# Two-layer encoder trunk: the feed-forward output product with four pairs of k-tiles by seven block products instead of eight, and its weight splits moved to VectorE

## What is computed

```python
def swiglu(x, w1, w3, w2):
    return (jax.nn.silu(x @ w1) * (x @ w3)) @ w2      # w1, w3: 1024 x 2816; w2: 2816 x 1024

for layer in range(2):
    mix = ...                                         # layer 0: chunk attention + state space; layer 1: stick-breaking attention
    h = layer_norm(ALPHA * h + mix, ln_mix_g[layer], ln_mix_b[layer])
    ffn = swiglu(h, ffn_w1[layer], ffn_w3[layer], ffn_w2[layer])
    h = layer_norm(ALPHA * h + ffn, ln_ffn_g[layer], ln_ffn_b[layer])
```

## Time and profile before

| | us |
|---|---|
| runs of the kernel | 1172.32, 1173.63, 1175.81 |
| median | 1173.63 |
| profiled execution, first to last instruction (span) | 1170.8 |
| PE busy in it | 1151.3 |
| DVE busy in it | 801.2 |
| POOL busy in it | 614.9 |
| output stage of layer 0, from the first to the last of its matmuls | 449.8 to 561.5 |
| output stage of layer 1 | 1043.6 to 1163.5 |

### The profile page before, as it was taken

How to read it: one execution, slowest core, us unless ns; L and a number is a source line. 1 busy time by engine, 2 the same in 40 slices (tenths; PEclk the granted TensorE clock), 3 DMA queues, 4 the chain that set the end, 5 groups by cost and what they waited for, 6 DMA issues and landing times.

```text
span 1170.8 us, 19103 instructions
## 1 busy us (share of the span) xinstructions
PE 1151.3 (98%) x7533; PEld 1003.2 (86%) x7533; DVE 801.2 (68%) x1064; ACT 514.5 (44%) x813; POOL 614.9 (53%) x384
## 2 busy tenths in 40 slices
PE   7999999999999999999999999999999999999997
PEld 6877768999999998888887777777999999998886
DVE  8558652897888887442804787756978888874427
ACT  6335674354544444222335555523544445543220
POOL 5897614356676767444353222213566776674440
PEclk9999999999999999999999999999999999999999
DMA  7623415143333334232243121202533333343211
GB/s 209 184 78 98 119 59 188 60 118 106 91 109 109 109 109 144 90 105 93 79 137 90 55 64 45 72 1 72 145 96 104 91 114 103 109 140 111 92 54 72
DMA packets 154201, 117.84 MB, mean 101 GB/s; under 512 B 19280, under 2 KB 140152, under 8 KB 154112
## 3 DMA queue, kind: packets, MB, share of 16 engines
q1 hardware_dynamic: 154112, 116.62, 33.3%
HBM read 113.17 MB, written 3.43 MB: 100 GB/s over the span
## 4 chain that ended last, share of the span: by engine, by line
PE 93%; DVE 4%; ACT 1%; DMA 1%; issue 0%; SPq 0%; POOL 0%; DVEq 0%; ACTq 0%
PE ps L1840 18%; PE ps L1841 17%; PE ps L1842 17%; PE ps L1862 10%; PE ps L1864 10%; PE ps L1863 10%; PE ps L2321 2%; PE ps L2347 2%; PE ps L2332 2%; PE ps L1870 1%; PE ps L2095 1%; PE ps L2365 1%; PE ps L2106 1%; PE ps L2367 1%; PE ps L2366 1%; PE ps L2119 1%
## 5 line engine op out<-in xcount | busy, mean ns | idle before, releaser
L693 POOL TENSOR_TENSOR wlo<-raw,whi 128x1024 fp32r<-128x1024 f32 x113 | 275.7, 2448 | 387.5 <-ACT whi L811 386.8
L1840 PE MATMUL ps<-xhi,whi 128*128 128x256 f32 (+1 forms) x848 | 272.3, 321 | 0.0
L1842 PE MATMUL ps<-xhi,wlo 128*128 128x256 f32 (+1 forms) x848 | 267.2, 315 | 0.0
L1841 PE MATMUL ps<-xlo,whi 128*128 128x256 f32 (+1 forms) x848 | 267.1, 315 | 0.0
L811 ACT CAST whi<-raw 128x1024 fp32r<-128x1024 f32 x113 | 120.1, 1075 | 190.8 <-PE ps L1864 160.4
L1840 PEld LDWEIGHTS ps<-xhi,whi 128*128 128x128 f32 x848 | 161.9, 191 | 17.4 <-issue 6.4
L772 POOL TENSOR_TENSOR wlo<-raw,whi 128x512 fp32r<-128x512 f32 x114 | 173.3, 1546 | 0.6 <-ACT whi L1077 0.4
L1842 PE MATMUL ps<-thi,wlo 128*128 128x256 f32 x608 | 172.4, 284 | 0.0
L1841 PE MATMUL ps<-tlo,whi 128*128 128x256 f32 x608 | 172.4, 284 | 0.0
L1840 PE MATMUL ps<-thi,whi 128*128 128x256 f32 x608 | 172.4, 284 | 0.0
L1842 PEld LDWEIGHTS ps<-xhi,wlo 128*128 128x128 f32 x848 | 161.8, 191 | 10.3
(11 more groups left out here) (253 smaller groups left out, 2008.2 us busy)
## 6 DMA issues: line engine op xcount, KB each, us to landing
raw<-in_ffn_w SPq DMA_DIRECT2D x132, 512.0 KB, 3.8
raw<-in_odd_w_in SPq DMA_DIRECT2D x24, 512.0 KB, 3.8
raw<-in_even_w_in SPq DMA_DIRECT2D x16, 512.0 KB, 4.6
h<-in_x SPq DMA_DIRECT2D x8, 512.0 KB, 5.3
raw<-in_even_w_out SPq DMA_DIRECT2D x8, 512.0 KB, 4.0
raw<-in_odd_w_out SPq DMA_DIRECT2D x8, 512.0 KB, 3.5
bias<-rel_scratch SPq DMA_DIRECT2D x8, 256.0 KB, 3.8
out<-h SPq DMA_DIRECT2D x3, 512.0 KB, 2.6
```

Source lines behind the costliest of these rows:

```text
L693: eng.tensor_tensor(lo, raw_of(b), hi, ALU.subtract).then_inc(w_lo, 1)
L1840: eng.matmul(o_, w_hi_, x_hi_, start=start, stop=False)
L1841: eng.matmul(o_, w_hi_, x_lo_, start=False, stop=False)
L1842: return eng.matmul(o_, w_lo_, x_hi_, start=False, stop=stop)
```

## The change

Of the 22 k-tiles of an output product, eight (0 to 7) are taken together: tiles 0 to 3 as the left and 4 to 7 as the right part of G (each pair of a left and a right tile is one of the four pairs), the tokens in two halves of 256, w2's columns in two halves of 512. The 2 x 2 block product then has seven block products P1 to P7 in place of eight. It is worked in two batches b of two pairs (JOINED = 4, BATCHES = 2), so there are 14 joint units of twelve matmuls. The matmuls of a product differ from plain ones only in their operands: sums of G blocks (`1s`, `3s`, `N`, `L`, 128 x 2 x 256) and of w2 blocks (`3t`, `1t`, `2t`, `4t`, 128 x 1024), all made by DVE; the w2 sums lie where x was, in `t1`, `t2`, `t3`. Where a product belongs to several outputs it is not kept aside: it is left in the PSUM bank of one of them and read into h by DVE at the right moment (`read_part`, eight reads of 128 x 512 a layer, with ALPHA * h in the same operation), and the next product is added to it in the same bank. The norm then adds h with factor 1.

The other 14 k-tiles stay plain. Ten (eight in layer 1) are taken as half units: A, two k-tiles for the left columns, and B, the same two for the right ones, with 24 matmuls each; the others are full units F of 24 matmuls as before. A product called 5b1 is P5 of batch 1.

The weight splits of this stage, and of no other, go from POOL to DVE (`out_lower`); ACT's half is `out_upper`. There are two more loads a layer, since the lower right blocks of w2 are loaded twice. Orders, and which sums DVE makes behind which unit:

```diff
+FIRST_UNITS = 3
+JOINED = 4
+OUT_ORDER = (
+    "A0 1b0 1b1 5b0 A1 5b1 A2 6b0 6b1 4b0 A3 2b0 A4 7b0 7b1 4b1 2b1 B0 3b0 B1 3b1 B2 B3 B4",
+    "A0 1b0 1b1 5b0 A1 5b1 6b0 A2 6b1 4b0 2b0 A3 7b0 7b1 4b1 2b1 B0 3b0 B1 3b1 B2 B3 F8")
+SUMS_BEHIND = (
+    {1: "N0 1s1 3s1", 2: "N1 3t0 1t0 2t0", 3: "3t1 1t1 2t1", 7: "4t0 L0", 8: "L1", 12: "4t1"},
+    {1: "N0 1s1 3s1", 2: "N1 3t0 1t0 2t0", 3: "3t1 1t1 2t1", 6: "4t0 L0", 8: "L1", 11: "4t1"})
```

```diff
+            kind, part = UNITS[layer][last - out_first(layer)]
+            if kind == P1:
+                sp_.wait_ge(t_sum, t_sum_upto(layer, f"2t{part}"))
+            if kind in (P2, P4):
+                sp_.wait_ge(t_sum, t_sum_upto(layer, f"4t{part}"))
...
+            def load_right(layer, b):
+                sp_.wait_ge(half_used, products_upto(layer, SEVENS - 1, P3))
+                for k0, store in ((JOINED + 2 * b, t3), (2 * b, t1)):
+                    eng.dma_start(store[:, 2 * b:2 * b + 2, :], tiles_of(w2[layer], k0 * P, S, S, 2)).then_inc(t_landed[b], 16)
```

POOL leaves these blocks out; in layer 0 its constant `newest` (a memset and a select) and its next splits wait:

```diff
-                split[0] = FFN[layer] + 2 * FT
+                split[0] = out_end(layer)
...
-            lower_upto(FFN[0] + 2 * FT + 4)
             pool.wait_ge(g_ready, FT)
+            pool.wait_ge(joint_lo, max(joint_upto(0, P5, b) for b in range(BATCHES)))
...
+            pool.wait_ge(w_lo, ordinary(out_end(0)))
```

ACT:

```diff
                     if i == SEVENS - 1:
-                        upper_upto(f + 2 * FT + 3)
-                g_upper(2)
...
+                        for u in range(FIRST_UNITS):
+                            out_upper(u)
+                for u in range(1, FIRST_UNITS):
+                    g_uppers(u)
+                for u in range(FIRST_UNITS, len(UNITS[layer])):
+                    g_uppers(u)
+                    out_upper(u)
```

DVE, behind the loop over the row pairs:

```diff
-                for j in range(2, FT):
-                    g_lower(j)
+                g_sums("1s", 0)
+                g_sums("3s", 0)
+                dve.wait_ge(w_lo, ordinary(out_first(layer)))
+                for u in range(len(UNITS[layer])):
+                    for p in read_before(layer, u):
+                        read_part(p)
+                    if u:
+                        g_lowers(u)
+                    out_lower(u)
+                    for name in SUMS_BEHIND[layer].get(u, "").split():
+                        ...
+                def out_lower(u):
+                    b_ = out_first(layer) + u
+                    dve.wait_ge(w_hi, ordinary(b_ + 1))
+                    tt(wlo[:, slot(b_), :], out_source(layer, u), whi[:, slot(b_), :].bitcast(F32), ALU.subtract).then_inc(w_lo, 1)
```

`g_lowers(u)` is the lower part of G for unit u: two tiles for an A, one joint part for a product, nothing for a B. PE:

```diff
+                def joint(u):
+                    kind, part = units[u]
+                    pe.wait_ge(w_lo, ordinary(first + u + 1))
+                    pe.wait_ge(joint_lo, joint_upto(layer, kind, part))
+                    if kind in (P6, P3, P7):
+                        pe.wait_ge(part_read, read_upto(layer, {P6: P1, P3: P5, P7: P6}[kind]))
+                    for k in range(2):
+                        for i, bank in enumerate(out_banks(kind)):
+                            mm = three_wide(ps[:, bank, :], ...)
+                    mm.then_inc(w_used, 1)
```

More of the change, by code:

```diff
@@ L99, in build, with unit_of @@
     PRODUCT_SLOTS = (PRODUCTS + 1) // 2
-    G_ORDER = list(range(16, FT)) + list(range(16))
+    FREE_TILES = 16
+    P1, P4, P2, P5, P6, P7, P3 = range(7)
+    HALF0, HALF1, FULL = "half 0", "half 1", "full"
+    BATCHES = JOINED // 2
+    G_ORDER = [16, 17] + list(range(2 * JOINED, FREE_TILES)) + list(range(18, FT))
+    G_PLAIN = len(G_ORDER)
+    TAILS = (TAIL, LAST_TAIL)
+    def unit_of(name):
+        if name[0] == "F":
+            return FULL, (int(name[1:]),)
+        if name[0] in "AB":
+            c = 2 * int(name[1:])
+            return HALF0 if name[0] == "A" else HALF1, (c, c + 1)
+        return (P1, P2, P3, P4, P5, P6, P7)[int(name[0]) - 1], int(name[2:])
+    UNITS = [[unit_of(name) for name in order.split()] + [(FULL, (j,)) for j in range(G_PLAIN - tail, G_PLAIN)]
+             for order, tail in zip(OUT_ORDER, TAILS)]
+    JOINT = [[unit for unit in row if unit[0] not in (HALF0, HALF1, FULL)] for row in UNITS]
+    GS = 7 * BATCHES
+    SUMS = ("3t", "1t", "2t", "4t"), ("1s", "3s", "N", "L")
     def ffn_blocks(layer):
-        FFN[layer] = len(blocks)
+        FFN[layer] = len(load_of)
         for m in range(PLAIN):
@@ L802, in upper_upto @@
                     b = rounded[0]
[L803 to L809, removed]
+                    act.wait_ge(*landed(b))
+                    slot_free(b)
                     hi = whi[:, slot(b), :]
@@ L1152, in _ @@
             norm(1, OV)
-            product(OV, KT)
+            for k in range(KT):
+                upper_upto(OV + k)
             upper_upto(OQK + 3)
@@ new lines, in read_part @@
+                def read_part(p):
+                    dve.wait_ge(w_used, ordinary(out_block(layer, p, BATCHES - 1) + 1))
+                    rows, half = {P1: (0, 0), P6: (0, 1), P7: (2, 0), P5: (2, 1)}[p]
+                    for i, bank in enumerate(out_banks(p)):
+                        into = h[:, rows + i, half * S:(half + 1) * S]
+                        eng.scalar_tensor_tensor(out=into, in0=into, scalar=ALPHA, in1=ps[:, bank, :], op0=ALU.mult,
+                                                 op1=ALU.subtract if p in (P1, P7) else ALU.add).then_inc(part_read, 1)
@@ L1856, in token_rows @@
             def token_rows(b, k, r, width, hi, lo, t, bank, n_half, start, stop, half0=0):
+                open_ = any(out_first(layer) <= b < out_end(layer) for layer in range(2))
                 c = slice(t * P, (t + 1) * P)
@@ L2259, in ffn, with ready @@
                 seventh(SEVENS - 1, P4)
[L2261 to L2268 removed]
+                units, first = UNITS[layer], out_first(layer)
+                def ready(u):
+                    pe.wait_ge(g_lo, plain_upto(layer, units[u][1][-1]))
@@ new lines, in plain_half @@
+                def plain_half(u):
+                    kind, part = units[u]
+                    half = kind == HALF1
+                    pe.wait_ge(w_lo, ordinary(first + u + 1))
+                    ready(u)
+                    if half:
+                        pe.wait_ge(part_read, read_upto(layer, P7))
+                    for ts in ((2, 3), (0, 1)):
+                        if u == 0 and ts == (0, 1):
+                            pe.wait_ge(g_ready, (layer + 1) * FT)
+                        for r, j in enumerate(part):
+                            w = slice(r * S, (r + 1) * S)
+                            for t in ts:
+                                c = slice(t * P, (t + 1) * P)
+                                mm = three_wide(ps[:, 2 * t + half, :], ghi[:, G_ORDER[j], c], glo[:, G_ORDER[j], c],
+                                                whi[:, slot(first + u), w], wlo[:, slot(first + u), w],
+                                                u == 0 and r == 0, False)
+                    mm.then_inc(w_used, 1)
@@ new lines, in plain_full @@
+                def plain_full(u):
+                    pe.wait_ge(w_lo, ordinary(first + u + 1))
+                    ready(u)
+                    for t in range(NT):
+                        mm = token_rows(first + u, G_ORDER[units[u][1][0]], 0, D, ghi, glo, t, 2 * t, 2, False, False)
+                    mm.then_inc(w_used, 1)
+                for u in range(len(units) - TAILS[layer]):
+                    kind = units[u][0]
+                    if kind in (HALF0, HALF1):
+                        plain_half(u)
+                    elif kind == FULL:
+                        plain_full(u)
+                    else:
+                        joint(u)
@@ L2270, in _ @@
+                place = {u: G_ORDER[units[u][1][0]] for u in range(len(units) - TAILS[layer], len(units))}
+                last_blocks(first, len(units), TAILS[layer], ghi, glo, 2 * layer + 1, ready, place)
             ffn(0)
```

302 lines of the change are left out of this document (237 added, 65 removed).

## The result

| | before | changed |
|---|---|---|
| median of the runs, us | 1173.7 | 1188.6 |
| lowest to highest | 1172.3 to 1175.8 | 1187.8 to 1189.7 |
| span of the profiled execution | 1170.8 | 1186.1 |

The changed kernel takes 1.0129 times as long, 95% interval 1.0115 to 1.0144: 14.9 us more, where 11.7 were forecast. The time lies inside the range.

What follows compares the result with a forecast made beforehand. PE, busy for 98% of the span, was taken to bound the kernel. Each layer: +11.3 us delay at A1, -5.4 for matmuls removed, +5.9; both layers +11.7, so 1173.6 becomes 1185.3 us, range 1176 to 1192.

Steps and rivals of the forecast that it cites:

- The price of a matmul: Output stage on PE: 0.2267 us per 512-column matmul, so 24 fewer save 5.44 us a layer, 10.9 us for both.
- The first stall: Start of the output stage: PE waits for DVE's split and starts A0 at 453.87 instead of 449.82, 4.05 us.
- The loads: SP's queue: 1b1's load, behind two right-hand loads, lands at 455.9, 7.3 us after the first issue; DVE stands until 457.6.
- DVE's list: DVE's operations from 1b0's G part to A1's weights: 17.0 us, ending at 474.6; the delay at A1 is 11.3 us.
- The waits one by one: PE early in the output stage: waits of 3 to 4 us before 5b0 and A1, released by DVE.
- No wait behind A1: Output stage after A1: DVE gets ahead of PE's 5.44 and 2.72 us units, so no later wait.
- Rival 1: Output stage: DVE's lists are covered and the 24 matmuls a layer come off whole, 1162.7 us; chance 0.06.
- Rival 2: Output stage: only the stall before A0 is real, the lists behind it hidden, -2.8 us, 1170.9; chance 0.08.
- Rival 3: Start of the output stage: loads are no hindrance and DVE never stands, +4.1 us, 1177.7; chance 0.12.
- Rival 4: TensorE's clock falls in the new gaps; before A1 this costs up to 3 us a layer, 1191; chance 0.08.
- POOL: Without POOL's splits, DVE's SBUF operations run at their own speed: a G split goes from 2.46 to 0.69 us.
- Span and median: Whole kernel: the median of the runs, 1173.6, lies 2.8 us over the profiled span, 1170.8, and moves by the same sum.

Runs made afterwards that it cites:

- the order alone: Changed kernel with only the units reordered (A0 A1 A2 1b0 1b1 5b0 5b1 A3 6b0 and so on), A0's weight split still on DVE: 1174.2 us.
- the run with the splits alone: Kernel before, with the output stage's weight splits moved to DVE, the first behind the last row's multiplication, and no block products: 1180.7 us.

## Why the prediction was right

- **The price of a matmul.** 0.2267 us, from the period of the casts. Right: 48 matmuls fewer, counted at 10.9 us, gave 9.8 and 11.6 us where nothing else stands in the way. The 131 ns of the Trainium skill ("TensorE: Matmul & The Clock Gate", "Back-to-back issue gap") would have given 6.3; both versions without waits contradict it.
- **The first stall.** Forecast 4.05, measured 4.0 in both layers. Right, and right that it is part of the delay at A1: with the split on POOL the time stayed at 1188.7.
- **The loads.** The step that was short. 1b1 was to land 7.3 us after the first issue of the burst; it landed 9.2 us after in layer 0 (449.86 to 459.05) and, from ACT's cast, some 8 in layer 1. Two things were not in the burst of the earlier trace rows that I took as the measure. One issue on SP's queue lasted 1.30 us (450.28 to 451.58, in layer 0 only). And two more loads follow the third at once: from 450 to 459 the DMA engines moved some 2.2 MB, where the three loads up to 1b1's are 1.6 MB, so they were at work on later ones before 1b1 had landed. The list therefore began at 460.69, which is 9.6 us after the seam, and not 7.8. That is 1.8 us in layer 0 and 0.7 in layer 1. The list itself was a little shorter than forecast, so A1 came 1.6 and 0.5 us later than forecast: 2.1 us of the 3.2 by which the sum fell short. The other 1.1 lie outside the stretch; in the profiled execution 1.3 us stand ahead of the stage, and the median of the kernel before varies by 0.7 from one set of runs to another (1173.0 to 1173.7). I took POOL's and DVE's rows with care and a DMA's landing from another kind of burst.
- **DVE's list.** Forecast 17.0 us; it took 16.9 (460.69 to 477.55). The operations are 0.60 and 1.14 us apart, as in the earlier trace rows. The G splits went from 2.46 to 0.68 us, as counted against the earlier trace rows.
- **The waits one by one.** Before 5b0 and before A1 PE was to wait 3 to 4 us. Before 5b0 it waited 2.73, but before A1 only 1.14 and 1.34: 5b0 itself ran mostly at half clock, 4.4 us in layer 0 instead of 2.72, and reached into that wait. The forecast of the waits had left this out; A1's time, set by DVE, did not move by it.
- **No wait behind A1.** Right: PE's 16.1 us of waits are seven, all at or before A1.
- **Rival 1** (faster, the matmuls come off whole) named the point from which it decides: A0's lower weights must be there at about 450. That was necessary, not sufficient. The versions that reach 1163.1 and 1162.0 needed the plain units first as well.
- **Rival 2** (only the first stall real) was forecast at 1170.9. The run that makes it true, the order alone, took 1174.2: 3.1 us of the difference were the clock, which that rival had left out.
- **Rival 3** (the loads no hindrance) was priced at 1177.7. The run that makes it true, 1b1's load first, took 1177.5. This bears out the forecast's account of DVE's list apart from the loads.
- **Rival 4** (the clock). Half right. The clock did fall, in the changed kernel twice in each layer (in A0, and in 5b0 after the wait before it), and it cost nothing there, since PE was still at A1 before DVE, by 1.14 and 1.34 us. The fall that would have cost, in the gap before A1, did not come: the clock was at 1.00 when A1 began. For the time it depends on whether the slow stretch is itself covered: 0 us in one order, 3.1 us in the other. The Trainium skill ("TensorE: Matmul & The Clock Gate", "Why this matters for your kernels") warns of the half clock after such gaps. After the first stall of 4 us the traces agree, in both layers of the changed kernel and of the run with the order alone.
- **POOL.** Right that DVE is faster without it. I had not said what would happen the other way round, and the run with all splits on POOL came out 3.5 us over its own range, in the main for that reason: PE's two longest waits for POOL, 7.24 and 7.52 us, are for the two splits that were held off.
- **Span and median.** I put 2.8 us between them; the runs that have both show 1.7 to 1.8. The rest was scatter of the kernel before, and it cancels in the difference.

## What to carry to other kernels

Removing work from the busiest engine pays only if the helpers' lists ahead of each unit are shorter than that engine's work so far. Lay both out from the seam, unit by unit, in program order: here a helper busy for some 70 us of a stage of 112 cost PE 25 us at the stage's start, where the helper first waited for a late load and then had 16.9 us of work against PE's 13.6. Put units with little preparation first, put a helper's first operation where it stands idle before the seam, and queue no early load behind one that must wait. Of several stalls on the way to one late point only the last counts, so mend them from that point backwards.

## What the runs showed of the hardware

- When DVE and POOL both work on two SBUF operands, the one that is already running holds the other off, and goes on doing so with its next operations where they follow without a pause. In the kernel before DVE waits for POOL (2.46 us for 0.68 us of work); in the run with all splits on POOL it is POOL that waits, 9.21 and 8.60 us for a split of 2.39, while DVE's operations keep their 0.68 and 1.21 us. Two DVE operations in that time that read PSUM (`h<-h,ps`) kept their length as well; the split's end, 2.2 us behind the last operation on two SBUF operands, says that it went on beside them.
- TensorE's clock, after PE had run out of matmuls, fell from 2.4 to 1.2 GHz: some 4.3 us after the last one in layer 0 of the changed kernel (451.3 to 455.6), about 2.1 us after it in the run with the splits alone (452.3 to 454.4), and 4.1 us after it at the end of the kernel before (1163.46 to 1167.6, the end in the earlier trace rows). It did not fall behind every such gap: behind the same wait of 2.65 us it stayed full in layer 1 of the run with the splits alone. In the changed kernel it was back at 459. Small transposes of the identity, 40 in 4.5 us, kept it up.
- Five loads of 512 KB issued within some 3 us share the DMA engines and land late: 7.1 us after the issue in the median for the right-hand ones, against 3.8 for the weight loads of the feed-forward blocks. In the busiest microsecond the engines moved 412 GB/s.
- The issue of the first two right-hand loads took SP's queue 1.71 us in layer 0 of the changed kernel and 0.88 in layer 1; in layer 0 of the runs with the other order of ACT, with the transposes and with all splits on POOL it took 2.03, 1.94 and 1.83 us, in that with the first split on POOL 0.88. Why stays open.
